# One decoder block in a single-core kernel: the windowed heads' values with the values stationary and the probabilities moving

## What is computed

```python
    s_band = jnp.einsum('bnqhgd,bnkhd->bnhgqk', qb, kb).astype(jnp.float32) * scale + bias_band[None, None]
    s_meta = jnp.einsum('bnqhgd,bmhd->bnhgqm', qb, km).astype(jnp.float32) * scale + bias_meta[None]
    ...
    p = jax.nn.softmax(jnp.concatenate([s_meta, s_band, sink], axis=-1), axis=-1)
    ...
    o = (jnp.einsum('bnhgqm,bmhd->bnqhgd', p_meta, vm)
         + jnp.einsum('bnhgqk,bnkhd->bnqhgd', p_band, vb))
    ...
        mix = jax.nn.sigmoid(ga) * (ya @ w_branch_a[l]) + jax.nn.sigmoid(gb) * (yb @ w_branch_b[l])
        h = h + rmsnorm(mix @ w_out[l], norm_attn_post[l])
        u = rmsnorm(h, norm_ff_pre[l])
        f = jnp.square(jax.nn.relu(u @ w_ff1[l])) @ w_ff2[l]
        h = h + rmsnorm(f, norm_ff_post[l])
```

## Time and profile before

| | us |
|---|---|
| time, median of 3 runs | 1438.92 |
| lowest and highest of them | 1435.8, 1439.13 |
| span of the profiled execution | 1431.9 |
| TensorE busy in it | 1406.0 (98%) |
| VectorE busy | 752.6 (53%) |
| ScalarE busy | 627.3 (44%) |

### The profile page before, as it was taken

The page is one execution under the profiler, slowest core; times in us unless marked ns, Lnnn a source line. Parts: engine busy times, 40 slices in busy tenths (PEclk is TensorE's granted clock), DMA queues, the critical chain, the costliest instruction groups (busy, mean ns, idle before and its releaser), DMA issues.

```text
span 1431.9 us, 18460 instructions
## 1 busy us (share of the span) xinstructions
PE 1406.0 (98%) x6859; PEld 1155.6 (81%) x6859; DVE 752.6 (53%) x960; ACT 627.3 (44%) x916; POOL 57.8 (4%) x87
## 2 busy tenths in 40 slices
PE   6999999999999999999899999999999999999997
PEld 6878877877778888888788888888888888888886
DVE  5543333345556555555666545565455654555654
ACT  5543234335455444445454433444334443344442
POOL 1231120000000000000000000000000000000000
PEclk9999999999999999999899999999999999999999
DMA  7765445355545666666466656665566655666662
GB/s 220 207 172 142 115 121 145 108 149 151 158 138 177 187 184 187 225 229 227 126 210 187 191 185 186 189 191 185 188 188 188 184 188 190 188 186 187 191 189 105
DMA packets 130405, 252.80 MB, mean 177 GB/s; under 512 B 8531, under 2 KB 11007, under 8 KB 129900
## 3 DMA queue, kind: packets, MB, share of 16 engines
q1 hardware_dynamic: 126448, 241.28, 55.5%
q0 software_dynamic: 2192, 4.74, 1.8%
q10 hardware_dynamic: 1676, 5.61, 1.1%
HBM read 249.43 MB, written 2.17 MB: 176 GB/s over the span
## 4 chain that ended last, share of the span: by engine, by line
PE 97%; ACT 1%; DMA 1%; DVE 1%; issue 0%; SPq 0%; DVEq 0%; ACTq 0%; POOLq 0%
PE bank L1087 21%; PE bank L1088 21%; PE bank L1089 21%; PE bank L1345 17%; PE bank L1347 9%; PE bank L1075 2%; PE bank L1231 1%; PE bank L1230 1%; PE bank L1099 1%; PE bank L1100 1%; DMA xs<-in_x 1%; PE bank L1192 1%; PE bank L1191 1%; ACT w_hi L349 0%; PE bank L1233 0%; ACT gate_b L397 0%
## 5 line engine op out<-in xcount | busy, mean ns | idle before, releaser
L678 DVE TENSOR_TENSOR w_lo<-raw,w_hi 128x1024 fp32r<-128x1024 f32 (+1 forms) x456 | 551.0, 1214 | 502.5 <-ACT w_hi L349 500.5
L349 ACT ACTIVATE w_hi<-raw 128x1024 fp32r<-128x1024 f32 (+1 forms) x456 | 474.0, 1050 | 520.0 <-DMA raw<-in_w_ff 385.4
L1345 PE MATMUL bank<-f_hl,w_hi 128*128 128x512 f32 x1024 | 362.4, 399 | 1.1 <-issue 1.1
L1347 PE MATMUL bank<-f_hl,w_lo 128*128 128x256 f32 x1024 | 285.8, 282 | 0.0
L1345 PEld LDWEIGHTS bank<-f_hl,w_hi 128*128 128x128 f32 x1024 | 192.5, 189 | 47.4 <-issue 2.0
L1087 PE MATMUL bank<-w_hi,u_hi 128*128 128x512 f32 (+1 forms) x544 | 216.9, 399 | 0.7 <-DVE w_lo L678 0.6
L1088 PE MATMUL bank<-w_lo,u_hi 128*128 128x512 f32 (+1 forms) x544 | 211.1, 388 | 0.0
L1089 PE MATMUL bank<-w_hi,u_lo 128*128 128x512 f32 (+1 forms) x544 | 210.9, 388 | 0.0
L1089 PE MATMUL bank<-w_hi,hid_lo 128*128 128x512 f32 x512 | 202.2, 395 | 0.0
L1088 PE MATMUL bank<-w_lo,hid_hi 128*128 128x512 f32 x512 | 202.2, 395 | 0.0
L1087 PE MATMUL bank<-w_hi,hid_hi 128*128 128x512 f32 x512 | 202.2, 395 | 0.0
(11 more groups left out here) (191 smaller groups left out, 1052.0 us busy)
## 6 DMA issues: line engine op xcount, KB each, us to landing
raw<-in_w_ff SPq DMA_DIRECT2D x256, 512.0 KB, 3.7
raw<-in_w_in SPq DMA_DIRECT2D x128, 512.0 KB, 3.7
raw<-in_w_out SPq DMA_DIRECT2D x32, 512.0 KB, 4.6
raw<-in_w_branch_b SPq DMA_DIRECT2D x16, 512.0 KB, 3.7
raw<-in_w_branch_a SPq DMA_DIRECT2D x16, 512.0 KB, 3.7
xs<-in_x SPq DMA_DIRECT2D x4, 512.0 KB, 9.7
raw<-in_w_in SPq DMA_DIRECT2D x8, 256.0 KB, 9.0
bias<-bias_table POOLq DMA_DIRECT2D x8, 256.0 KB, 4.6
```

Of the source, the lines that this page charges most:

```text
L349: act.activation(w_hi[:, u, :, 0:width], raw[:, u, :, 0:width], ACT.Copy).then_inc(hi_ready, 1)
L678: dve.tensor_tensor(w_lo[:, u, :, 0:width], raw[:, u, :, 0:width], w_hi[:, u, :, 0:width].bitcast(F32), ALU.subtract).then_inc(lo_ready, 1)
L1345: both = lambda: pe.matmul(acc[g][:], w_hi[:, u, k, cols], f_hl[:, kt, :], start=kt == 0, stop=kt == KT - 1)
L1347: low = lambda: pe.matmul(acc[g][:, 0:SEQ], w_lo[:, u, k, cols], f_hl[:, kt, 0:SEQ], start=False, stop=False)
```

## The change

The values of a windowed job change their operands' places. The stationary operand is now the values (64 columns), the moving one the transposed probabilities, 256 positions at a time. The result lies with the features in the partitions: head e = 0 in partitions 0 to 63, e = 1 in 64 to 127 of S1, columns 256 to 511. The products are written in the order meta, first key block, second key block, each for both heads in turn. As positions are now along the columns, the reciprocals can't be applied at the eviction; `job_combine` scales the probabilities in `t` before they are transposed, behind a linked reciprocal. `job_keep_out` becomes a plain copy into a new tile `yT`, and `y` loses its second half. The four turns of the second branch's columns fall away (`UNTURNED = 4` is taken off the counts that others wait for), and `keep_y` splits those columns straight from `yT`. The first branch is unchanged.

```diff
@@ scalar, keep_y
                 g = (i + 4) % 8
+                if g >= 4:
+                    act.wait_ge(o_ready, JOBS)
+                    act.wait_ge(o_kept, HB // 2)
+                    act.activation(y_hi[:, 2 * g:2 * g + 2, :], yT[:, 2 * g - 8:2 * g - 6, :], ACT.Copy)\
+                       .then_inc(turned_hi, 1)
+                    return
@@ vector, job_combine
                 dve.wait_ge(exp_done, j + 1)
+                link(dve.reciprocal(rs, sums))
                 if j < HB // 2:
-                    dve.reciprocal(rs, sums).then_inc(probs_ready, 1)
+                    n0 = P + META + 1
+                    for e in range(2):
+                        for q, (a, b) in enumerate(((1, n0), (n0 + 1, 2 * n0 + P))):
+                            i = 2 * e + q
+                            last = dve.tensor_scalar(t[:, e, a:b], t[:, e, a:b], rs[:, i:i + 1], None, ALU.mult)
+                    last.then_inc(probs_ready, 1)
                     return
-                link(dve.reciprocal(rs, sums))
@@ vector, job_keep_out
                 if j < HB // 2:
-                    c0 = HA * P + j * P
-                    dst = y[:, :, c0:c0 + P].rearrange("p q (e d) -> p q e d", e=2)
-                    src = S1[:, 2 * P:4 * P].rearrange("p (q e d) -> p q e d", q=2, e=2)
-                    r = rs.rearrange("p (e q a) -> p q e a", e=2, a=1).broadcast_to([P, 2, 2, DHB])
+                    dve.tensor_copy(yT[:, j, :], S1[:, 2 * P:4 * P]).then_inc(o_kept, 1)
+                    return
@@ vector, keep_y
                 g = (i + 4) % 8
+                if g >= 4:
+                    dve.wait_ge(turned_hi, T_Y + i + 1)
+                    dve.tensor_tensor(y_lo[:, 2 * g:2 * g + 2, :], yT[:, 2 * g - 8:2 * g - 6, :],
+                                      y_hi[:, 2 * g:2 * g + 2, :].bitcast(F32), ALU.subtract)\
+                       .then_inc(turned_lo, 1)
+                    return
@@ tensor, job_values
+                if windowed:
+                    col = slice((j // 4) * DHB, (j // 4 + 1) * DHB)
+                    o = [S1[e * DHB:(e + 1) * DHB, 2 * P:4 * P] for e in range(2)]
+                    for e in range(2):
+                        pe.matmul(o[e], vb_m[:, col], pTm[:, e, :], start=True, stop=False)
+                    for e in range(2):
+                        pe.matmul(o[e], vb[:, 0, col], pT[:, e, 0:2 * P], start=False, stop=False)
+                    for e in range(2):
+                        ins = pe.matmul(o[e][:, P:], vb[:, 1, col], pT[:, e, 2 * P:3 * P], start=False, stop=True)
+                    ins.then_inc(o_ready, 1)
+                    return
@@ tensor, turn_y and mix_pair
-                if i >= 2:
+                if i >= 6:
                     pe.wait_ge(turned_lo, T_Y + i - 1)
...
-                        turn_y(u)
+                        if u >= UNTURNED:
+                            turn_y(u)
```

More of the change, by code:

```diff
@@ L79 @@
 T_Y = 8
+UNTURNED = 4
 T_M = T_Y + 8
@@ L146, in hybrid_block @@
             [("f_hl", [P, KT, 2 * SEQ], F32R)])
-        (y, t, pT, pTm, bias), (m_hi, m_lo), (hid_hi, hid_lo), (xs,) = region(
+        (y, yT, t, pT, pTm, bias), (m_hi, m_lo), (hid_hi, hid_lo), (xs,) = region(
             2 * KT * SEQ,
-            [("y", [P, BLOCKS, 2 * HA * P], F32), ("t", [P, 2, 418], F32), ("pT", [P, 2, 3 * P], F32),
+            [("y", [P, BLOCKS, HA * P], F32), ("yT", [P, HB // 2, SEQ], F32), ("t", [P, 2, 418], F32), ("pT", [P, 2, 3 * P], F32),
              ("pTm", [META, 2, 2 * P], F32), ("bias", [P, 2, 2, 418], F32)],
@@ L356, in keep_hi @@
             def keep_hi(n, dst, src, scale=None):
-                act.wait_ge(turned, n + 1)
+                act.wait_ge(turned, n + 1 - UNTURNED)
                 if scale is None:
@@ L628, in quarter @@
                             if first and j == 1:
-                                act.wait_ge(turned, T_F)
+                                act.wait_ge(turned, T_F - UNTURNED)
                             else:
@@ L838, in job_keep_out @@
                 if j < HB // 2:
-                    c0 = HA * P + j * P
-                    dst = y[:, :, c0:c0 + P].rearrange("p q (e d) -> p q e d", e=2)
-                    src = S1[:, 2 * P:4 * P].rearrange("p (q e d) -> p q e d", q=2, e=2)
-                    r = rs.rearrange("p (e q a) -> p q e a", e=2, a=1).broadcast_to([P, 2, 2, DHB])
[L843 to L847, removed]
+                    dve.tensor_copy(yT[:, j, :], S1[:, 2 * P:4 * P]).then_inc(o_kept, 1)
+                    return
+                h = j - HB // 2
+                dst = y[:, :, h * P:(h + 1) * P]
+                src = MB[:, P:3 * P].rearrange("p (q d) -> p q d", q=2)
+                r = rs[:, 0:2].rearrange("p (q a) -> p q a", a=1).broadcast_to([P, 2, P])
                 dve.tensor_tensor(dst, src, r, ALU.mult).then_inc(o_kept, 1)
@@ L964, in new_stream @@
                 if j >= 2:
-                    dve.wait_ge(turned, T_H + 2 * (j - 1))
+                    dve.wait_ge(turned, T_H + 2 * (j - 1) - UNTURNED)
                 for b in range(BLOCKS):
@@ L1218, in job_values @@
                 pe.wait_ge(pTm_kept, j + 1)
[L1219 to L1233, removed]
+                if windowed:
[9 more added lines that the diff above has]
+                    return
+                h = j - HB // 2
+                col = slice(h * P, (h + 1) * P)
+                vm, vr = va_m[:, col], [va[:, b, col] for b in range(BLOCKS)]
+                for q in range(2):
+                    o = MB[:, P + q * P:P + (q + 1) * P]
+                    pe.matmul(o, pTm[:, 0, q * P:(q + 1) * P], vm, start=True, stop=False)
+                    ins = pe.matmul(o, pT[:, 0, q * P:(q + 1) * P], vr[0], start=False, stop=q == 0)
+                    if q == 1:
+                        ins = pe.matmul(o, pT[:, 0, 2 * P:3 * P], vr[1], start=False, stop=True)
                 ins.then_inc(o_ready, 1)
```

## The result

The changed kernel takes 1415.0 us (median of 4 runs, 1414.0 to 1415.6) against 1438.8 us before (1435.8 to 1439.1): ratio 0.984, 95% interval 0.982 to 0.986. The two traces, however, are only 18.1 us apart. Of these, 17.9 lie between the first scores (the first L1191 matmul, L1208 in the changed kernel) and the fifth turn of y, the first that is left: this stage takes 358.6 us before and 340.7 after.

The account below looks back on a forecast made before the run. TensorE was taken to bound the kernel; values 13.9, turns 1.8 and low clock 1.5 sum to 17.2 us, taking the span from 1431.9 to 1414.7, plus 7.0 around it: 1421.7 us, eight-in-ten range 1419.5 to 1428.5.

Parts of the forecast that it names:

- the bound and the path: Whole kernel: TensorE busy 98% of the span, 97% of the last-ending chain, without waits from 60 to 600 us.
- 12 at least: Stage from first scores to last y turn: the forecast counts as wrong if it shrinks by less than 12 us.
- the values: TensorE's value insertions in eight windowed jobs: 3.39 us becomes 1.65 each, gaining 13.9 us (13.2 to 15.5).
- side by side with covered loads: Windowed values: both heads run at once with weight loads hidden, as forecast; 1421.7 us, chance 0.76.
- the lower end: Value insertion: smaller loads and a way out near 0.05 instead of 0.22 us would give 1.45 us.
- rival 3: Windowed values: one half runs after the other, 2.72 us per job; 1430.2 to 1431.7 us, chance 0.09.
- Rival 2: Windowed values: heads side by side but loads not covered, 4.8 us in all; about 1426.5 us, chance 0.10.
- the turns: First mix pair on TensorE: turn_y runs four times instead of eight, 0.45 us each, gaining 1.8 us.
- the scalings: VectorE in job_combine: four scalings and a linked reciprocal add 1.3 us, at most 1.7, within 2.56 us slack; no cost.
- the slower rival: Windowed values: halves in turn plus a low clock behind every job's insertion; 1442 us, chance 0.02.
- the base of the sum: Whole kernel: profiled span 1431.9 us plus 7.0 us around it, kept unchanged, against the median of 1438.92.
- the low clock: Behind the fifth value insertion, 200 to 203 us: the half-clock fall goes, gaining 1.5 us (bounds 0 and -1.5).

Follow-up runs that it names:

- the second trace: The kernel before, run once more with no edit to get another trace: 1438.5 us (1436.2 to 1439.6, eight runs).

## Why the prediction was right and where it was wrong

**Right: the bound and the path.** Between the traces, 17.9 of 18.1 us came out of the stage with TensorE's insertions (the prediction wanted 12 at least), and TensorE still waits for nothing between 60 and 600 us.

**Right: the values.** Forecast side by side with covered loads, 1.65 us in 1.45 to 1.74 (the pieces of the lower end add up to 1.47, which changes nothing); measured 1.57. The scores were the right row to take the concurrency from, and rival 3 would have been 2.72; the kernel with both heads in one half measured 2.64, so its price was right as well. Rival 2 does not occur. Weight loads (PEld) of the changed kernel, first job's values:

```profile
91.30 0.36 PEld L1244 LDWEIGHTS bank<-pT,vb 128*64 128x64 f32 x4
```

These loads begin at 91.30, while the last 256-column passes stream until the 128-column ones start at 91.51, on the same 128 rows. That contradicts in divided columns too the second rule cited from the Trainium skill, that loads overlap only with passes of other row groups. The first, on the speed of column tiles, the runs bear out in kind, for two tiles of 64 columns: passes that take 2.14 us in one half take 1.07 in two.

**Right: the turns** (0.45 us each) **and the scalings** (they use 1.07 us of the slack against 1.3, and leave 1.49). The mechanism of the slower rival, falls behind insertions in half an array, did not show: an insertion of 5.1 us in half the columns brought none, in its trace or by the clock of its six runs.

**Wrong: the base of the sum.** The failed step is "Around it lie 7.0 us against the median of the runs (1438.92); that I keep". Around the span lie 1.8 us, in every run of either kernel that lists its span. The other 5.2 were time at half clock that the profiled execution happened not to have, and the change takes it away with the one fall that was there. (The four runs of before in the result list neither span nor clock; this is read from the forty later ones of that kernel, whose medians lie at 1436.0 to 1438.5 us, and from the second trace.) The term "the low clock" had the mechanism right (it took the one fall as gone, since the run of short passes shrinks and gets denser) and the size wrong: 1.5 us where the ordinary execution had about 6.7 to lose, the 1.5 and the 5.2. With that, 17.2 + 5.2 = 22.4 us and 1416.5, 1.5 from the measured time; 0.7 of these are in the values, forecast at 13.9 and measured at 14.6. The bounds of this term, 0 to 1.5 and -1.5, looked only at what the one trace showed. There was a hint: the runs spread over 3.3 us, from 1435.8 to 1439.1, as much as two such falls.

**Left over.** Outside the stage the traces differ by 0.2 us: the changed kernel reaches its first scores 0.8 us later, and needs 1.0 less from TensorE's wait near 690 us to the end, where the low stretch was 10 us long before and 7 after. Two traces of the changed kernel differ by 1.4 us in the first of these and by 0.4 in the second, so it means nothing.

## What to carry to other kernels

If the runs are several microseconds above the profiled span, find out whether that gap is the same for every execution before it is carried over; a wide spread of the runs and a granted clock below the profile's say that it is a part of the kernel. Work with 64 output columns gained here by making the 64-wide operand stationary and running two heads in two halves of the columns, written so that no change in the number of rows lies between what should run together. Products that contract over few rows belong next to each other: each change between 16 and 128 rows cost 0.13 to 0.19 us here.

## What the runs showed of the hardware that was not expected

- The granted clock fell to 1.2 GHz although the profile shows TensorE busy without a gap (240.00 of 240.00 us). What preceded it were runs of 64-column fp32 passes with changes of rows between, in insertions of 3.4 us (also 2.85 us); two pieces of 1.7 us with 1.4 us of big matmuls between did not bring it, nor did 2.9 or 5.1 us of passes of 256 and 128 columns in half of the array at a time.
- Whether a given insertion brings a fall differs from execution to execution of the same kernel: one of eight in one trace, three of eight in the next. The length of a low stretch differs too, 3.4 or 6.8 us.
- Two halves of the columns run together also where a product of the other half stands between them in the program, but not across a change between 16 and 128 rows: 1.58 us against 2.92 for the same six products.
